# Sliding-window attention in a two-block kernel: fused bias and maximum, softmax weights normed on GpSimd before their transposition, value products laid out by feature and split straight from PSUM

## The reference

```python
def block_attn(args):
    qb, kk, vv, blk = args
    s = jnp.einsum('bqkgd,bskd->bkgqs', qb, kk) + bias
    valid = band & ((blk > 0) | (kj >= B_BLOCK))
    s = jnp.where(valid, s, -jnp.inf)
    m = jnp.maximum(jnp.max(s, axis=-1), sink)
    p = jnp.exp(s - m[..., None])
    denom = jnp.sum(p, axis=-1) + jnp.exp(sink - m)
    o = jnp.einsum('bkgqs,bskd->bqkgd', p, vv)
    return o / jnp.transpose(denom, (0, 3, 1, 2))[..., None]
...
return o.astype(h.dtype) @ w_o + b_o
```

## Time and profile before

| | us |
|---|---|
| median of three executions | 2332.92 |
| lowest, highest | 2331.96, 2337.13 |
| span of the profiled execution, first to last instruction | 2331.1 |
| PE busy in it | 2185.5 (94%) |
| DVE busy | 1202.5 (52%) |
| ACT busy | 827.5 (35%) |
| POOL busy | 111.7 (5%) |
| chain that ended last, share of PE | 75% |

### The profile page before, as it was taken

The page is one execution under the profiler, slowest core; times in us unless marked ns, Lnnn a source line. Parts: engine busy times, 40 slices in busy tenths (PEclk is TensorE's granted clock), DMA queues, the critical chain, the costliest instruction groups (busy, mean ns, idle before and its releaser), DMA issues.

```text
span 2331.1 us, 30145 instructions
## 1 busy us (share of the span) xinstructions
PE 2185.5 (94%) x11768; PEld 1558.0 (67%) x11768; DVE 1202.5 (52%) x1801; ACT 827.5 (35%) x1508; POOL 111.7 (5%) x139
## 2 busy tenths in 40 slices
PE   6999999889999999798988999999999899999997
PEld 3788757633334333366775988888887677888885
DVE  4799676410000000358757447778435654877822
ACT  3222343223333323344563433223323553222421
POOL 0000000031111011100012000000000000000000
PEclk9999999989999999899998899999999899999999
DMA  9442203589999998712211112222233103223221
GB/s 388 180 162 92 72 37 119 242 343 426 427 427 423 421 423 360 281 37 72 73 37 37 37 73 76 105 108 77 104 109 139 43 1 109 76 105 108 78 103 72
DMA packets 34455, 384.62 MB, mean 165 GB/s; under 512 B 8112, under 2 KB 8384, under 8 KB 11456
## 3 DMA queue, kind: packets, MB, share of 16 engines
q1 hardware_dynamic: 27520, 374.96, 40.5%
q0 software_dynamic: 6848, 8.45, 1.0%
HBM read 382.59 MB, written 14.73 MB: 170 GB/s over the span
## 4 chain that ended last, share of the span: by engine, by line
PE 75%; DMA 12%; DVE 8%; ACT 3%; issue 2%; SPq 0%; DVEq 0%; ACTq 0%; POOL 0%; POOLq 0%
PE PS L654 18%; PE PS L656 18%; PE PS L655 18%; DMA A<-wexp 10%; PE PS L882 7%; PE PS L891 2%; PE PS L927 2%; DVE A L1955 1%; PE PS L1058 1%; DMA x<-xt_in 1%; PE PS L607 1%; PE PS L972 1%; PE PS L614 1%; PE PS L1279 1%; PE PS L634 0%
## 5 line engine op out<-in xcount | busy, mean ns | idle before, releaser
L655 PE MATMUL PS<-h_r,w_hi_r 128*128 128x512 f32 (+1 forms) x1088 | 422.1, 388 | 0.0
L654 PE MATMUL PS<-h_hi_r,w_hi_r 128*128 128x512 f32 x1024 | 411.7, 402 | 9.1 <-DVE h_r L2615 3.0
L656 PE MATMUL PS<-h_hi_r,ring_r 128*128 128x512 f32 x1024 | 400.3, 391 | 0.0
L2265 DVE TENSOR_TENSOR ring_r<-ring,w_hi_r 128x1024 fp32r<-128x1024 f32 x192 | 233.7, 1222 | 320.6 <-ACT w_hi_r L1543 320.5
L1543 ACT ACTIVATE w_hi_r<-ring 128x1024 fp32r<-128x1024 f32 x192 | 202.0, 1058 | 554.2 <-PE PS L656 319.9
L655 PEld LDWEIGHTS PS<-h_r,w_hi_r 128*128 128x128 f32 x1088 | 205.8, 189 | 45.8 <-issue 5.2
L654 PEld LDWEIGHTS PS<-h_hi_r,w_hi_r 128*128 128x128 f32 x1024 | 193.5, 189 | 61.9 <-issue 11.0
L656 PEld LDWEIGHTS PS<-h_hi_r,ring_r 128*128 128x128 f32 x1024 | 193.6, 189 | 41.0
L882 PE MATMUL PS<-A 128*64 128x512 f32 x768 | 176.6, 613 | 23.5 <-DMA A<-wexp 21.5
L1955 DVE SCALAR_TENSOR_TENSOR A<-A,vec 128x511 f32<-128x511 f32 (+15 forms) x216 | 160.1, 741 | 6.7
L2250 DVE TENSOR_TENSOR A<-A,PS 64x256 f32<-64x256 f32 x16 | 6.6, 412 | 280.1 <-ACT A L1519 280.1
(11 more groups left out here) (486 smaller groups left out, 3466.8 us busy)
## 6 DMA issues: line engine op xcount, KB each, us to landing
A<-wexp SPq DMA_DIRECT2D x64, 2048.0 KB, 16.8
ring<-wall SPq DMA_DIRECT2D x63, 2048.0 KB, 8.1
ring<-wexp SPq DMA_DIRECT2D x16, 2048.0 KB, 18.1
h<-wexp SPq DMA_DIRECT2D x16, 2048.0 KB, 20.1
A<-wada SPq DMA_DIRECT2D x12, 2048.0 KB, 15.7
x<-xt_in SPq DMA_DIRECT2D x2, 2048.0 KB, 11.4
A<-y_assignments SPq DMA_DIRECT2D x4, 1024.0 KB, 8.0
h_tokens<-A SPq DMA_DIRECT2D x4, 512.0 KB, 3.0
```

The lines of the kernel that those rows point to most:

```text
L654: mm(out, w[0], x_[0], start=first, stop=False)
L655: mm(out, w[0], x_[1], start=False, stop=False)
L656: return mm(out, w[1], x_[0], start=False, stop=last_)
L2265: tt(ring_r[:, slot, :, cols], ring[:, slot, :, cols], w_hi_r[:, :, cols].bitcast(F32), ALU.subtract).then_inc(S("w_lo"), 1)
```

## The change

- `maxima(u)`: bias and maximum are one DVE operation per head, `tensor_tensor_reduce`. It writes the negated sum of score and bias, and accumulates its minimum, which begins with the negated sink; `sinks` are negated once beforehand. ACT's exponential takes the negated sum with a scale of -1. The separate reductions 2597, 2599 and 2600 are gone. Each such operation comes out as two instructions, the main one and one of 128x1 that writes the accumulator out.
- GpSimd multiplies the weights of each unit by the reciprocal of their denominator, in place, before they are transposed. PE's transposes now wait for it (`at_pn`) where they waited for ACT's exponentials (`at_p`).
- The copy of the transposed weights from PSUM moves from ACT to DVE (`weights_out`), after the reciprocal.
- `values(u)` has the values as stationary operand and the transposed weights as moving one: the product comes out by feature. The heads of a unit lie in two pairs on partitions 0 to 63 and 64 to 127. `rows_scaled`, `rows_out` and `features_out` are gone.
- The hi and lo parts are made from PSUM, unit by unit (`features_hi` on ACT, `features_lo` on DVE, three steps behind).
- PE takes the scores of the pair after the next one after `values`, where it took those of the next pair ahead of `weights_T`.

```diff
--- before.py
+++ after.py
@@ -261,7 +261,7 @@
 ...
-        sm = [sb(f"sm{i}", [P, 4, AH // KVH]) for i in range(4)]
+        sm = [sb(f"sm{i}", [P, 4, AH // KVH]) for i in range(3)]
         ATT = NT * KVH
 ...
@@ -272,8 +272,14 @@
         def pT_buf(u):
             return A[:, 46 + 2 * (u % 2):48 + 2 * (u % 2), :]
-        def o_rows(u):
-            return A[:, 50 + u % 2, 0:256]
+        def by_row(v):
+            return v.rearrange("p a (b c d) -> p (a b) c d", c=2, d=P)
+        def features(u):
+            return slice(2 * (u % KVH), 2 * (u % KVH) + 2), slice(P * (u // KVH), P * (u // KVH + 1))
+        def features_ps(u):
+            return PS[:, 6 + u % 2, 0:2 * P].rearrange("p (a b) -> p a b", b=P)
 ...
@@ -1258,7 +1264,7 @@
             def weights_T(u):
-                pe.wait_ge(S("at_p"), u + 1)
+                pe.wait_ge(S("at_pn"), u + 1)
                 if u:
                     pe.wait_ge(S("at_pt"), u)
                 for i in range(4):
@@ -1272,35 +1278,25 @@
                 b, g = u // KVH, u % KVH
                 pe.wait_ge(S("at_pt"), u + 1)
                 if u >= 2:
-                    pe.wait_ge(S("at_o"), u - 1)
-                for i in range(4):
-                    for kk in range(0 if b else 1, 2):
-                        n, t = 2 * i + kk, b - 1 + kk
-                        last = mm(PS[:, 6 + u % 2, i * HD:(i + 1) * HD], pT_buf(u)[:, n // 4, (n % 4) * P:(n % 4 + 1) * P],
-                                  A[:, 10 + t // 2, 256 * (t % 2) + g * HD:256 * (t % 2) + (g + 1) * HD], start=kk == 0 or not b, stop=kk == 1)
+                    pe.wait_ge(S("at_lo"), u - 1)
+                for kk in range(0 if b else 1, 2):
+                    t = b - 1 + kk
+                    for i in range(2):
+                        last = mm(PS[HD * i:HD * (i + 1), 6 + u % 2, 0:2 * P], A[:, 10 + t // 2, 256 * (t % 2) + g * HD:256 * (t % 2) + (g + 1) * HD],
+                                  by_row(pT_buf(u))[:, i:4:2, kk, :], start=kk == 0 or not b, stop=kk == 1)
                 last.then_inc(S("at_pv"), 1)
-            def rows_out(u):
-                pe.wait_ge(S("at_on"), u + 1)
-                for i in range(2):
-                    last = nc.tensor.transpose(PS[:, 6 + u % 2, 256 + i * P:256 + (i + 1) * P], o_rows(u)[:, i * P:(i + 1) * P], ident)
-                last.then_inc(S("at_ot"), 1)
 ...
             scores(0)
+            scores(1)
             for u in range(ATT):
-                if u % 2 == 0 and u + 2 < ATT:
-                    scores(u // 2 + 1)
                 weights_T(u)
-                if u >= 2:
-                    rows_out(u - 2)
                 if u:
                     values(u - 1)
+                if u % 2 == 0 and u + 4 < ATT:
+                    scores(u // 2 + 2)
             values(ATT - 1)
-            rows_out(ATT - 2)
-            rows_out(ATT - 1)
 ...
@@ -1786,23 +1782,17 @@
             def exps(u):
-                act.wait_ge(S("at_m"), 2 * u + 2)
+                act.wait_ge(S("at_m"), u + 1)
                 link(a_(sm[2][:, u % 4, :], sm[2][:, u % 4, :], ACT.Exp))
                 for i in range(4):
-                    last = a_(p_buf(u)[:, i, :], p_buf(u)[:, i, :], ACT.Exp, bias=sm[0][:, u % 4, i:i + 1], accum_out=sm[1][:, u % 4, i:i + 1])
+                    last = a_(p_buf(u)[:, i, :], p_buf(u)[:, i, :], ACT.Exp, scale=-1.0, bias=sm[0][:, u % 4, i:i + 1], accum_out=sm[1][:, u % 4, i:i + 1])
                 last.then_inc(S("at_p"), 1)
-            def features_out(u):
-                b, g = u // KVH, u % KVH
-                act.wait_ge(S("at_ot"), u + 1)
-                a_(h[:, 2 * g:2 * g + 2, b * P:(b + 1) * P], PS[:, 6 + u % 2, 256:512].rearrange("p (a b) -> p a b", b=P), ACT.Copy).then_inc(S("at_o"), 1)
-            def block_hi(b):
-                cols = slice(b * P, (b + 1) * P)
-                act.wait_ge(S("at_o"), KVH * (b + 1))
-                a_(h_hi_r[:, :, cols], h[:, :, cols], ACT.Copy).then_inc(S("h_hi"), 2)
+            def features_hi(u):
+                act.wait_ge(S("at_pv"), u + 1)
+                done = (S("at_hi"), 1) if u < ATT - 1 else (S("h_hi"), KD)
+                a_(h_hi_r[:, features(u)[0], features(u)[1]], features_ps(u), ACT.Copy).then_inc(*done)
             for j in range(4):
                 w_hi(UIDX["w_o0"], j)
@@ -1810,20 +1800,10 @@
             for u in range(ATT):
                 if u + 1 < ATT:
                     exps(u + 1)
-                act.wait_ge(S("at_t"), u + 1)
                 if u >= 2:
-                    act.wait_ge(S("at_pv"), u - 1)
-                src, dst = PS[:, 4:6, :], pT_buf(u)
-                if not u // KVH:
-                    src, dst = (v.rearrange("p a (b c d) -> p (a b) c d", c=2, d=P)[:, :, 1, :] for v in (src, dst))
-                a_(dst, src, ACT.Copy).then_inc(S("at_pt"), 1)
-                if u >= 2:
-                    features_out(u - 2)
-                if u >= 6 and u % KVH == 2:
-                    block_hi(u // KVH - 1)
-            features_out(ATT - 2)
-            features_out(ATT - 1)
-            block_hi(NT - 1)
+                    features_hi(u - 2)
+            features_hi(ATT - 2)
+            features_hi(ATT - 1)
             for j in range(4):
 ...
             for j in range(3):
@@ -2587,36 +2567,39 @@
                 dve.wait_ge(S("at_s"), u // 2 + 1)
                 if u >= 4:
                     dve.wait_ge(S("at_t"), u - 3)
-                    dve.wait_ge(S("at_on"), u - 3)
                 src = PS[:, 2 * (u % 2):2 * (u % 2) + 2, :].rearrange("p a (b c) -> p (a b) c", c=256)
                 bias = A[:, 12 + 2 * g:14 + 2 * g, :].rearrange("p a (b c) -> p (a b) c", c=256)
                 if not u // KVH:
                     src, bias = src[:, :, P:256], bias[:, :, P:256]
-                tt(p_buf(u), src, bias, ALU.add).then_inc(S("at_a"), 1)
+                sinks = R("sinks")[:, 4 * g:4 * g + 4]
+                for i in range(4):
+                    last = nc.vector.tensor_tensor_reduce(out=p_buf(u)[:, i, :], in0=src[:, i, :], in1=bias[:, i, :], scale=-1.0, scalar=sinks[:, i:i + 1],
+                                                          op0=ALU.add, op1=ALU.min, accum_out=sm[0][:, j, i:i + 1])
+                last.then_inc(S("at_a"), 1)
                 dve.wait_ge(S("at_a"), u + 1)
-                link(nc.vector.tensor_reduce(sm[3][:, j, :], p_buf(u), AX, ALU.max))
-                sink = R("sinks")[:, 4 * g:4 * g + 4]
-                link(tt(sm[3][:, j, :], sm[3][:, j, :], sink, ALU.max))
-                ts(sm[0][:, j, :], sm[3][:, j, :], -1.0, None, ALU.mult).then_inc(S("at_m"), 1)
-                tt(sm[2][:, j, :], sink, sm[3][:, j, :], ALU.subtract).then_inc(S("at_m"), 1)
-            def rows_scaled(u):
-                dve.wait_ge(S("at_pv"), u + 1)
-                if u >= 2:
-                    dve.wait_ge(S("at_ot"), u - 1)
-                tt(o_rows(u).rearrange("p (a b) -> p a b", b=HD), PS[:, 6 + u % 2, 0:256].rearrange("p (a b) -> p a b", b=HD),
-                   sm[1][:, u % 4, :].rearrange("p (a b) -> p a b", b=1).broadcast_to([P, 4, HD]), ALU.mult).then_inc(S("at_on"), 1)
-            def block_lo(b):
-                cols = slice(b * P, (b + 1) * P)
-                dve.wait_ge(S("h_hi"), KD * h_sets[0] + 2 * (b + 1))
-                tt(h_r[:, :, cols], h[:, :, cols], h_hi_r[:, :, cols].bitcast(F32), ALU.subtract).then_inc(S("h_lo"), 2)
+                tt(sm[2][:, j, :], sm[0][:, j, :], sinks, ALU.subtract).then_inc(S("at_m"), 1)
+            def features_lo(u):
+                dve.wait_ge(*((S("at_hi"), u + 1) if u < ATT - 1 else (S("h_hi"), KD * (h_sets[0] + 1))))
+                done = (S("at_lo"), 1) if u < ATT - 1 else (S("h_lo"), KD)
+                tt(h_r[:, features(u)[0], features(u)[1]], features_ps(u), h_hi_r[:, features(u)[0], features(u)[1]].bitcast(F32), ALU.subtract).then_inc(*done)
             for j in range(4):
                 w_lo(UIDX["w_o0"], j)
+            link(ts(R("sinks"), R("sinks"), -1.0, None, ALU.mult))
             dve.wait_ge(S("bias"), 16)
+            def weights_out(u):
+                dve.wait_ge(S("at_t"), u + 1)
+                if u >= 2:
+                    dve.wait_ge(S("at_pv"), u - 1)
+                src, dst = PS[:, 4:6, :], pT_buf(u)
+                if not u // KVH:
+                    src, dst = (by_row(v)[:, :, 1, :] for v in (src, dst))
+                cp(dst, src).then_inc(S("at_pt"), 1)
             maxima(0)
             maxima(1)
             for u in range(ATT):
@@ -2624,13 +2607,15 @@
                     maxima(u + 2)
                 dve.wait_ge(S("at_p"), u + 1)
                 link(tt(sm[1][:, u % 4, :], sm[1][:, u % 4, :], sm[2][:, u % 4, :], ALU.add))
-                link(nc.vector.reciprocal(sm[1][:, u % 4, :], sm[1][:, u % 4, :]))
+                nc.vector.reciprocal(sm[1][:, u % 4, :], sm[1][:, u % 4, :]).then_inc(S("at_r"), 1)
                 if u:
-                    rows_scaled(u - 1)
```

(15 more changed lines are left out.)

## The result

The changed kernel took 2337.18 us in the median of 12 runs (2332.61 to 2339.6), the kernel before 2332.5 of 12 (2327.89 to 2337.13): ratio 1.0020 [1.0012, 1.0028], so 4.7 us slower. The forecast was 9.3 us slower. The sign and the cause of the loss were right; the size was twice too large, above all because a gain behind the stage was put at nothing.

The account below looks back on a forecast made before the run. It took the attention stage as critical, DVE leading at 8.10 us a pair, then a GpSimd loop of 8.41. Full clock summed to 0, clock +8.3 and +1: +9.3 us, 2342.2 us; forecast's own range 2337 to 2346, overall 2330 to 2350.

Parts of the forecast that it names:

- up to unit 4's maxima: Stage's start: negating sinks adds 0.2 us, and scores queued behind the first transposes come about 1.0 us later.
- five pairs: Steady part: 40.4 us against 40.5 at full clock by the loop over GpSimd, plus 8.3 us for the clock.
- from unit 14's maxima to the output projection: Stage's end: about 18.0 us instead of 18.9, 0.9 less, with 1 us added for the clock.
- The 2.5 us behind the stage stay as they are.: Start of the output projection: the 2.5 us lost to half clock over its first 5.0 us remain.
- rival A: The clock holds despite PE's pauses in the stage: 2330 to 2335 us, no change; chance 0.20.
- The fused operation: DVE's bias and minimum per head: 0.48 us with the accumulator's read, 2.00 a unit; bounds 0.34 and 0.63.
- case C: Rival: accumulator's read does not overlap, 0.63 us a head, pairs of 9.0, with the clock +14: 2347 us; chance 0.13.
- the clock's +1: Last two units, where transposes and products are on the chain: 1 us added for half clock.
- 1.67: Clock loss in us a pair: 45% of the loop's 3.7 us of PE work; 8.3 us for five pairs.
- The collision of GpSimd with DVE: DVE operations with two SBUF inputs meet GpSimd's multiply only in the last two steps: some 0.6 us, contained in the 18.0.
- gives nothing by itself: ACT loses a copy of about 1 us and two smaller ones; not ahead in the loop, so no gain.
- rival B: Faster: accumulator's read free on DVE, 0.34 us a head, and the clock holds: -6.8 us, 2326; chance 0.13.

Follow-up runs that it names:

- e4: The kernel before with 20 transposes of a constant on PE in its last pause, ahead of the output projection: 2331.62 us, ratio 0.9992 [0.9983, 1.0001].
- e6: The changed kernel with two DVE copies that nobody reads ahead of the last lo part, to lengthen PE's last pause: 2339.4 us, ratio 1.0031.
- e1: The changed kernel with PE repeating one unit's scores in the pauses ahead of the transposes of units 2 to 12: 2329.82 us, ratio 0.9985.
- e2: The changed kernel with sum and reciprocal of a unit moved ahead of the maxima of unit u + 2 on DVE: 2321.96 us, ratio 0.9954.
- e3: The changed kernel without GpSimd's multiply, so the softmax weights are not divided by their sum: 2324.55 us, ratio 0.9965.
- e9: The changed kernel with the reciprocal ahead of the maxima and odd units' copies on ACT (last unit's on DVE): 2315.22 us, ratio 0.9927.
- e11: The kernel of e2 run again, as the reference for e9 on the same chip: 2321.25 us, ratio 0.9957.
- e7: The changed kernel with the reciprocal ahead of the maxima and the copies of even units on ACT: 2321.1 us, ratio 0.9955.
- e5: The kernel before with only the fused bias and maximum operation (exponential scale -1, sinks negated): 2327.53 us, ratio 0.9978.

## Why the prediction was right and wrong

Term by term, against the trace of before (forecast, measured):

| stretch | forecast | measured |
|---|---|---|
| up to unit 4's maxima | +1.0 | -0.1 |
| five pairs | +8.2 | +7.9 |
| from unit 14's maxima to the output projection | +0.1 | -1.5 |
| behind the stage | 0 | -2.3 |
| ahead of the stage (untouched code) | 0 | +0.7 |
| sum | +9.3 | +4.6 |

The measured first term is 1841.30 - 1824.62 = 16.68 against 1840.70 - 1823.92 = 16.78. The third is 1907.00 - 1889.66 = 17.34 against 1900.06 - 1881.20 = 18.86. Behind the stage it is 2335.7 - 1907.00 = 428.7 against 2331.1 - 1900.06 = 431.0. The +0.7 is the later start of the scores, well inside the 5.5 us by which that start differs between the traces of this document.

- **The step that failed: "The 2.5 us behind the stage stay as they are."** They did not. The forecast had itself listed their return as possible, under rival A ("if PE's shorter last pauses save the half clock behind the stage"), and left it out of its sum. The stage's new end, one unit's hi and lo part instead of a block's, leaves PE 1.07 us of pause instead of 2.95, and the clock stays at 2.4 GHz. e4 shows the same from the other side: the kernel before with this pause filled starts the projection at 1.00. e6 shows the reverse: the changed kernel with a pause of 2.46 falls to 0.51 there. This is 2.3 of the 4.7 us by which the sum was too large, about half.
- **The fused operation** was taken at 2.00 us a unit, and took 1.74. The read of the accumulator has no slot of its own. A head costs 0.41, half way between the 0.48 taken and the bound of 0.34, and just the 0.40 from start to start of the row nearest in form. The Trainium skill, page "VectorE: DVE Perf Modes", section "The DRAIN you can't avoid", has the next operation wait for an empty pipe, unless nothing holds it, and the prediction took from it that the read would wait (case C). In this trace the read and the next fused operation start together at 1880.13, 0.07 before the end (1880.20) of the operation ahead: nothing held them, and case C did not occur. The shorter operation gives 0.5 of the 1.6 us by which the end of the stage was overestimated, in two units. Nearly all the rest is the clock's +1, the second term that was not there: over 1889.7 to 1907.0 the clock was 1.00. At the start of the stage it gives three sets of 0.26, 0.8 of the 1.1; the rest was not separated.
- **The five pairs** came out as forecast, loop and clock, in part by luck. The loop without the clock is, from the rows above, with the products at full clock as in e1 (1866.76 to 1867.77) and the scores as there (1867.77 to 1869.82): reciprocal to GpSimd 0.26, multiply to transposes 1.95, transposes 1.02, products 1.01, scores 2.05, fused operations, subtraction and sum 2.01: 8.30, the 8.3 that e1 leaves when it takes the clock away. The forecast was 8.41, with the fused operations and what follows them 0.29 too dear and the products 0.16 too cheap. In the pair of 1875.03 the products took 1.90 from start to start and the scores 2.79, 1.6 more than at full clock (forecast 1.67), which makes 9.93, the pair's measured time (1869.79 to 1879.72). That 1.67 was 45% of PE's 3.7 us in the loop, a share picked between 41% and 61% of another stage. It came out at 44%, but nothing in the forecast derives it for this loop: the mechanism was right, the size was a fortunate choice.
- **The pause and its cure.** The pause was forecast at 2.8 and is 2.23, still enough. That GpSimd is not dear in itself is shown by e2 beside e3: with its multiply and without it the pairs are 7.5. What costs is that the reciprocal stands behind the next maxima, in a loop that PE closes with the transposes. The collision of GpSimd with DVE was as forecast: one at the end, in which `L2609` takes 0.62 instead of 0.15 us.

```profile
1896.78 0.62 DVE L2609 TENSOR_TENSOR sm<-sm 128x4 f32<-128x4 f32 x1
```

- **ACT "gives nothing by itself"** was right for the list of the changed kernel, but it hid what the move of the copy did: ACT was idle for nearly half of the five pairs (25.76 busy of 48.40 us), DVE got the work, and e9 gains by giving half of the copies back.
- **A slip** in rival B: three sets of 0.56 make 1.7 us, not 1.5. It changes nothing.

## What to carry to other kernels

When a change puts a third engine between two that alternate, write down the loop over all of them and ask which instruction of it can go earlier in its own list. Here two lines in another order turned +4.7 us into about -11 against the kernel before, and then moving one copy in two gave 6 more (e9 beside e11, on one chip). Which copy mattered: the same saving on the same list gave nothing in e7 and 6 us in e9, since only one of the two stood in the loop.

Where PE's pauses change, work out the clock for each of them, those that get shorter too. A forecast that charges the clock for new pauses and leaves the old one at its old price counts one side only.

## What the runs showed of the hardware

- PE pauses and granted clock: with pauses of 2.23 us in every pair, about 3.4 us near half clock in each of the last three (0.58, 0.55 and 0.54; 1.6 lost a pair); after 2.95 us at the stage's end 0.50 for the 5 us shown (before and e5); after 2.46 half clock for 3.4 us, beginning 0.8 us after PE had started again; after 1.07 at the stage's end 1.00; with pauses of 1.27 and below in every pair 1.00 throughout the steady part (e2, e1, e9). It isn't a matter of the pause alone: in e4 the clock fell to 0.56 behind pauses of 0.59 and 0.42.
- On one chip the kernel before took 2326.49 to 2335.86 us (17 runs) and e9 2314.78 to 2315.92 (5 runs): the spread is not the same for all versions. Whether the clock makes it was not tested.
- A minimum over 256 elements beside the main operation has no slot of its own on DVE: 0.41 us from one operation to the next for 128x256 with PSUM, SBUF and a pointer as inputs (0.40 for the nearest operation without one), and 0.27 for 128x128.
- GpSimd multiplies 128x1024 in place by a broadcast column in 1.89 us in all full units, and some 0.06 us lie from its end to PE's start. Beside it a DVE operation of 128x4 with both inputs in SBUF took 0.62 us instead of 0.15 (changed kernel), and 0.23 to 0.31 instead of 0.16 (e2).
